# A hybrid encoder trunk on one Trainium2 core: neighbourhood outputs by features, probabilities normalised on GpSimd

## The reference

```python
s = jnp.einsum('brqhd,brkwhd->bhrqkw', qg, k_band).astype(jnp.float32) * (d ** -0.5) + bias
s = jnp.where(in_win[:, None, :], s, -jnp.inf)
p = jax.nn.softmax(s.reshape(B, H, rows, GRID_W, kh * GRID_W), axis=-1).reshape(s.shape)
o = jnp.einsum('bhrqkw,brkwhd->brqhd', p.astype(v.dtype), v_band)
...
mixed = jnp.concatenate([ml_out, na_out, gla_out], axis=-1).astype(h.dtype)
return mixed @ w_out
```

## Time and profile before

| | |
|---|---|
| time, median of 3 runs | 879.58 us (879.28 to 880.8) |
| the profiled execution's own time | 878.24 us |
| its span | 876.3 us |
| TensorE matmul busy | 861.8 us, 98% of the span |
| VectorE busy | 596.0 us, 68% |
| ScalarE busy | 496.1 us, 57% |
| GpSimd busy | 14.3 us, 2% |
| granted TensorE clock, mean | 0.998 of full speed |

### The profile page before, as it was taken

How to read it: one execution, slowest core, us unless ns; L and a number is a source line. 1 busy time by engine, 2 the same in 40 slices (tenths; PEclk the granted TensorE clock), 3 DMA queues, 4 the chain that set the end, 5 groups by cost and what they waited for, 6 DMA issues and landing times.

```text
span 876.3 us, 14948 instructions
## 1 busy us (share of the span) xinstructions
PE 861.8 (98%) x6338; PEld 798.1 (91%) x6338; DVE 596.0 (68%) x820; ACT 496.1 (57%) x689; POOL 14.3 (2%) x35
## 2 busy tenths in 40 slices
PE   8999999999999999999999999999999899999997
PEld 8999998889889999999999999988898899999996
DVE  6887678757657666666577885887665666656655
ACT  7954663658647445445567546745755645445444
POOL 5000000000000000000000000000000000000000
PEclk9999999999999999999999999999999999999999
DMA  9735452364255555555448254335435365555541
GB/s 329 201 102 177 156 178 103 112 226 144 97 193 190 195 190 195 192 191 194 145 140 257 72 171 165 127 115 192 135 109 191 127 212 190 193 196 190 192 169 48
DMA packets 114665, 146.78 MB, mean 168 GB/s; under 512 B 10600, under 2 KB 94760, under 8 KB 114600
## 3 DMA queue, kind: packets, MB, share of 16 engines
q1 hardware_dynamic: 114456, 145.57, 49.7%
q10 hardware_dynamic: 144, 0.26, 0.1%
HBM read 144.77 MB, written 1.05 MB: 166 GB/s over the span
## 4 chain that ended last, share of the span: by engine, by line
PE 92%; ACT 3%; DVE 3%; issue 1%; DMA 0%; ACTq 0%; DVEq 0%
PE bank L665 26%; PE bank L666 25%; PE bank L667 25%; PE bank L706 4%; PE bank L743 2%; PE bank L832 2%; DVE wlo L1455 2%; PE bank L1017 2%; ACT whi L1096 1%; ACT yhi L1119 1%; PE bank L872 1%; PE bank L762 1%; PE bank L849 1%; DVE ylo L1710 1%; PE bank L882 1%
## 5 line engine op out<-in xcount | busy, mean ns | idle before, releaser
L1455 DVE TENSOR_TENSOR wlo<-raw,whi 128x2048 fp32r<-128x2048 f32 (+3 forms) x144 | 306.2, 2133 | 106.1 <-ACT whi L1096 105.2
L1096 ACT ACTIVATE whi<-raw 128x2048 fp32r<-128x2048 f32 (+3 forms) x144 | 257.4, 1793 | 53.5 <-PE bank L667 48.4
L665 PE MATMUL bank<-yhi,whi 128*128 128x256 f32 x704 | 195.1, 277 | 0.5 <-DVE ylo L1471 0.5
L666 PE MATMUL bank<-ylo,whi 128*128 128x256 f32 x704 | 194.6, 276 | 0.0
L667 PE MATMUL bank<-yhi,wlo 128*128 128x256 f32 x704 | 194.6, 276 | 0.0
L665 PEld LDWEIGHTS bank<-yhi,whi 128*128 128x128 f32 x704 | 132.2, 188 | 1.6 <-issue 0.7
L666 PEld LDWEIGHTS bank<-ylo,whi 128*128 128x128 f32 x704 | 132.2, 188 | 0.8
L667 PEld LDWEIGHTS bank<-yhi,wlo 128*128 128x128 f32 x704 | 132.2, 188 | 0.0
L665 PE MATMUL bank<-xhi,whi 128*128 128x256 f32 x320 | 91.4, 286 | 2.2 <-DVE wlo L1455 1.2
L665 PE MATMUL bank<-whi,xhi 128*128 128x512 f32 (+2 forms) x256 | 90.1, 352 | 0.0
L667 PE MATMUL bank<-xhi,wlo 128*128 128x256 f32 x320 | 88.9, 278 | 0.0
(11 more groups left out here) (268 smaller groups left out, 1373.1 us busy)
## 6 DMA issues: line engine op xcount, KB each, us to landing
raw<-in_w_up SPq DMA_DIRECT2D x44, 1024.0 KB, 5.0
raw<-in_w_down SPq DMA_DIRECT2D x22, 1024.0 KB, 4.8
raw<-in_w_in SPq DMA_DIRECT2D x10, 1024.0 KB, 7.3
raw<-in_w_xk SPq DMA_DIRECT2D x8, 1024.0 KB, 5.1
raw<-in_w_xv SPq DMA_DIRECT2D x8, 1024.0 KB, 4.9
raw<-in_w_out SPq DMA_DIRECT2D x8, 1024.0 KB, 4.8
raw<-in_w_xq SPq DMA_DIRECT2D x8, 1024.0 KB, 5.7
raw<-in_w_xo SPq DMA_DIRECT2D x8, 1024.0 KB, 4.9
```

Of the source, the lines that this page charges most:

```text
L665: mm(o, s_hi, m_hi, start=first, stop=False, skip_group_check=True)
L666: mm(o, s_hi, m_lo, start=False, stop=False, skip_group_check=True)
L1096: A(weight(whi, gu), raw[:, gu % RING, 0:SIZE[gu]], ACT.Copy).then_inc(hi_done, 1)
L1455: tt(weight(wlo, gu), raw[:, gu % RING, 0:SIZE[gu]], weight(whi, gu), ALU.subtract).then_inc(lo_done, 1)
```

## The change

A head's output is computed with the operands swapped: the values are the stationary side (64 columns), the transposed probabilities the moving one (256 columns), so that the result has features on the partitions. Two heads share a bank, one on the lower and one on the upper 64 partitions. There are three such groups in place of five: heads 0 and 1 at hh 3, heads 2 and 3 at hh 5, head 4 at hh 6 (`NA_OUT`, `NA_PAIRS`). Each stands ahead of the transposes of its `hh`. Their results are split straight from the bank into `yna_hi` (ScalarE) and `yna_lo` (VectorE), which are operands of the projection for feature groups 3, 4 and the lower half of 5. So groups 3 and 4 are no longer turned through `tmb`, and the projection begins with group 3.

Since a token's sum can no longer be applied per partition of the output, the probabilities are divided before they are transposed. VectorE takes the reciprocal of the sums (`shares_of`), GpSimd multiplies the two halves of the head's probabilities in place (two instructions of 128 by 256), and TensorE's transposes wait for GpSimd (`npn_ready`) where they waited for ScalarE. GpSimd's program after its constants is these 20 multiplications and their waits.

VectorE's order changes too. The mLSTM heads' finish (`heads_sum`) moves from hh 0 to hh 2: ahead of the reciprocals of heads 2 and 3 in layer 0, behind them in layer 1. The unit `xk1` (layer 0) or `xk3` (layer 1) is split at hh 0, ahead of the scores of heads 2 and 3, and on ScalarE it moves ahead of the second `gg` copy. ScalarE's two exponentials for the GLA move from hh 1 to hh 2, behind the heads' own.

```diff
@@ layer_events
     for h in range(NAH + 2):
+        if h in NA_OUT:
+            p = NA_OUT.index(h)
+            job(f"nao{p}", 4 + p % 2)
         if 1 <= h <= NAH:
             job(f"nat{h - 1}", 2 + (h - 1) % 2)
-        if h >= 2:
-            job(f"nao{h - 2}", 4 + (h - 2) % 2)
...
+NA_OUT = (3, 5, 6)
+NA_PAIRS = ((0, 1), (2, 3), (4,))
+NA_K = range(3, 6)
...
+        MIXED_K = (0, 1, 2, 5, 6, 7)
...
@@ gpsimd
+            for l in range(DEPTH):
+                for i in range(NAH):
+                    pool.wait_ge(nsum_ready, NAH * l + i + 1)
+                    for t in range(TT):
+                        last = g.tensor_scalar(np_[:, i % 2, t, :], np_[:, i % 2, t, :], nsum[:, 2 * i + t:2 * i + t + 1], None, ALU.mult)
+                    last.then_inc(npn_ready, 1)
...
@@ tensor
                 for hh in range(NAH + 2):
+                    if hh in NA_OUT:
+                        p = NA_OUT.index(hh)
+                        is_drained(pe, l, f"nat{NA_PAIRS[p][-1]}")
+                        free(f"nao{p}")
+                        for jt in range(TT):
+                            for g in NA_PAIRS[p]:
+                                r = slice(64 * (g % 2), 64 * (g % 2) + 64)
+                                last = mm(bank(f"nao{p}")[r, 0:T], nav[:, jt, g * DH:(g + 1) * DH], npt[:, g % 2, jt].rearrange("p a b -> p (a b)"),
+                                          start=jt == 0, stop=jt == 1, skip_group_check=True)
+                        last.then_inc(te_done, 1)
                     if 1 <= hh <= NAH:
                         g = hh - 1
-                        pe.wait_ge(np_ready, NAH * l + g + 1)
+                        pe.wait_ge(npn_ready, NAH * l + g + 1)
...
-                    if hh >= 2:
-                        g = hh - 2
-                        is_drained(pe, l, f"nat{g}")
-                        free(f"nao{g}")
-                        for t in range(TT):
-                            for jt in range(TT):
-                                last = mm(bank(f"nao{g}")[:, t * DH:(t + 1) * DH], npt[:, g % 2, t, jt, :],
-                                          nav[:, jt, g * DH:(g + 1) * DH], start=jt == 0, stop=jt == 1)
...
                     for k in (i, i + 4):
+                        if k not in MIXED_K:
+                            continue
                         for t in range(TT):
                             last = nc.tensor.transpose(turned_bank(l, "mx", k)[:, t * P:(t + 1) * P], tmb[:, t, k * P:(k + 1) * P], ident[:])
                     last.then_inc(te_done, 1)
-                for n in range(2):
-                    tm_unit(f"wo{n}", (f"wo{n}0", f"wo{n}1"), 512, "mx", n == 0)
+                tm_half("wo0", "a", ("wo00", "wo01"), 512, "mx", True, ks=(3,), first=3, ends=None)
+                tm_half("wo0", "a", ("wo00", "wo01"), 512, "mx", True, ks=(0, 1, 2), first=3, ends=2)
+                tm_half("wo0", "b", ("wo00", "wo01"), 512, "mx", True)
+                tm_unit("wo1", ("wo10", "wo11"), 512, "mx")
...
@@ vector
+                def shares_of(g):
+                    dve.wait_ge(np_ready, NAH * l + g + 1)
+                    V.reciprocal(nsum[:, 2 * g:2 * g + 2], nsum[:, 2 * g:2 * g + 2]).then_inc(nsum_ready, 1)
+
+                def heads_lo(p):
+                    dve.wait_ge(na_hi_ready, 3 * l + p + 1)
+                    r = slice(0, 64 * len(NA_PAIRS[p]))
+                    drain(tt(forwards(yna_lo[r, p, :]), backwards(bank(f"nao{p}")[r, 0:T]), forwards(yna_hi[r, p, :]), ALU.subtract))
...
                     if hh == 2:
+                        if l == 0:
+                            heads_sum()
+                        for g in NA_PAIRS[1]:
+                            shares_of(g)
                         if l:
-                            split_lo("xk3")
+                            heads_sum()
+                        else:
+                            split_lo("xk2")
+                        dve.wait_ge(eb_ready, 2 * l + 2)
...
                         if l == 0:
                             split_lo("xk3")
+                        heads_lo(0)
                     if hh == 4 and l == 0:
                         head_squares(mlh, sq, 0, MLH)
                     if hh == 4:
+                        shares_of(4)
                         split_lo("xv0a")
-                    if hh == 5 and l:
-                        head_squares(mlh, sq, 0, MLH)
+                    if hh == 5:
+                        if l:
+                            head_squares(mlh, sq, 0, MLH)
+                        heads_lo(1)
```

More of the change, by code:

```diff
@@ L335, in build @@
             eg = mixer.enter_context(nc.sbuf_tensor("eg", [P, TT, GV], F32))
+        with ExitStack() as mixer:
+            yna_lo = mixer.enter_context(nc.sbuf_tensor("yna_lo", [P, 3, T], F32R))
         chi = sb("chi", [P, KT, T], F32R)
@@ L712, in fm_unit, with input_is, tm_half @@
                     fm_blocks(name, group, [(f, 0, KT) for f in range(WCOLS[UNIT[l, name]] // P)], fresh, stepped=stepped)
-                def tm_half(unit, half, names, n, group, fresh=False, tokens=(0, 1), ks=range(4)):
+                def input_is(group, kk):
+                    if group == "mx" and kk in NA_K:
+                        is_drained(pe, l, f"nao{kk - 3}")
+                    if group != "mx" or kk in MIXED_K:
+                        lo_is(pe, l, group, kk)
+                def tm_half(unit, half, names, n, group, fresh=False, tokens=(0, 1), ks=range(4), first=0, ends=3):
                     have((l, unit + half))
                     hi, lo = weights((l, unit + half), 4)
-                    x = PAIR[group]
                     for t in tokens:
-                        if half == "a":
+                        if half == "a" and ks[0] == first:
                             free(names[t])
@@ L723, in tm_half @@
                             if fresh and t == 0:
-                                lo_is(pe, l, group, kk)
+                                input_is(group, kk)
                             s = slice(t * P, t * P + P)
+                            x = operand(group, kk)
                             way = from_the_end if unit in ("xv1", "xw1") and t == TT - 1 and kk == KT - 1 else (lambda v: v)
-                            last = split_mm(way(bank(names[t])[:, 0:n]), x[0][:, kk, s], x[1][:, kk, s],
-                                            way(hi[:, k, :]), way(lo[:, k, :]), kk == 0, kk == KT - 1)
-                        if (half == "b" or t == TT - 1) and k == 3:
+                            last = split_mm(way(bank(names[t])[:, 0:n]), x[0][:, s], x[1][:, s],
+                                            way(hi[:, k, :]), way(lo[:, k, :]), kk == first, kk == KT - 1)
+                        if (half == "b" or t == TT - 1) and k == ends:
                             last.then_inc(te_done, 1)
@@ L1271, in _ @@
                         memory_hi("mem", l, range(4, KT))
+                        split_hi("xk3" if l else "xk1")
                         take("gg1")
```

97 lines of the change are left out of this document (47 added, 50 removed).

## The result

| | before | after |
|---|---|---|
| median of the runs, us | 879.43 (879.26 to 880.8, 4 runs) | 892.99 (892.54 to 894.48, 4 runs) |
| ratio to before, 95% interval | | 1.015 [1.0135, 1.0166] |
| profiled execution, us | 878.24 | 892.75 |
| its span, us | 876.3 | 891.0 |
| mean granted clock of TensorE | 0.998 | 0.989 |

What follows compares the result with a forecast made beforehand. TensorE, busy 98% of the span, was taken to bound the kernel. Losses 3.6 + 2.9 less 2 x (0.44 + 0.30) gave +5.0: profiled 878.24 becomes 883.2, median 884.6 us; range 879 to 888.

Steps and rivals of the forecast that it cites:

- three places: TensorE's transposes wait for GpSimd at head 2 in layer 0 (1 to 2 us), head 4 in both layers (about 2 and 5).
- TensorE's saving: Head outputs in the loop: 4.05 us a layer falls to 2.9, saving 1.15; 4.1 in all if nothing new waited.
- The four transposes and the wait for `wo0b`: At the projection, four transposes fewer save 0.44 us a layer and the wait for the split of `wo0b` 0.30.
- The multiplication: GpSimd, ahead of each head's transposes: 0.42 us each, from a select's row; 0.9 for a head's two.
- The hold: A GpSimd instruction started inside a VectorE split (2.2 us) with two SBUF inputs gets nothing done until it is over.
- The walk of VectorE: VectorE's steps through the loop; with GpSimd free, layer 0 gains 0.7 us and layer 1 loses 1.9 at `kt0`.
- +2.9: Layer 0's loop: `kt0` at 142.0 where it was 139.09, a loss of 2.9 us.
- +3.6: Layer 1's loop: `kt0` at 571.8 where it was 568.18, a loss of 3.6 us.
- the free GpSimd: Rival: GpSimd is not held, so 2.2 us behind each split fall away; 879.3 us, chance 0.12.
- a won race: Rival: GpSimd gets a multiplication in ahead of the split, or both ahead of the squares; 882.5 us, chance 0.14.
- The slow multiplication: Rival: a GpSimd multiplication takes 0.85 us, not 0.42, adding 3.3; 888 us, chance 0.13.

Runs made afterwards that it cites:

- experiment 1: The changed kernel without the division: GpSimd's 20 multiplications gone, TensorE's transposes wait for the exponentials; 881.14 us, ratio 1.0021 to the kernel before.
- experiment 8: The changed kernel with the multiplications on VectorE and VectorE's work in another order; 876.16 us, ratio 0.9962 to the kernel before.
- Experiment 7: The changed kernel with each GpSimd multiplication cut to 64 of its 256 columns, so the output differs; 885.74 us, ratio 1.0076 to the kernel before.
- experiment 4: The changed kernel, but VectorE waits for head 2's and head 4's multiplications before it goes on; 887.44 us, ratio 1.0105 to the kernel before.
- experiment 6: The kernel before with only GpSimd's division added and reciprocals early; outputs and other order as before; 900.98 us, ratio 1.0245 to the kernel before.

## Why the prediction was too low

Its direction and its three places were right, and its mechanism as far as it went. What failed is the size of two terms: a wait was priced at its length alone, with nothing for the clock behind it, which measured 4.9 us; and a multiplication was put at 0.42 and measured 0.92, and its hold at what was left of the split, and it lasted longer. The steps, in its order:

**TensorE's saving: right in sum, a little high in the loops and low at the projections.** In experiment 1 layer 0's loop is 0.73 shorter with 0.35 of waiting for the split of `xk2` in it (transposes to `xk2` 0.76 for 0.41), so 1.08 was saved for 1.15. In experiment 8 it is 0.72, its wait left out: the filling ahead of an output group is longer than it was (6 products 0.93 for 0.79, 18 products 2.25 for 2.16), and transposes take 0.53 ahead of scores, where before they took 0.44 ahead of outputs. It seems that a step between products of different tile shapes costs about 0.1 here, which the forecast had near nothing; no run was made for it. Head 4's output takes 1.01, from 148.25 to 149.26, where 0.9 was forecast, and in experiment 8 a pair's takes 1.01 too (123.76 to 124.77; forecast 1.0). The four transposes and the wait for `wo0b` were put at 0.74 a layer; the change shows 1.15 and 1.20. In layer 1 of experiment 8 the twelve transposes take 1.23 to the next product where sixteen took 1.78, that is 0.55 and not 0.44, and the wait of 0.30 had stood in a step of 0.68 between two products that otherwise follow after 0.23, so 0.45 went with it.

**The multiplication: mis-sized.** Priced at 0.42 from a select of the same extent; it takes 0.92. This lies outside the bounds of 0.18 to 0.85 too. A row of another operation with the same shape was no price. Experiment 7 shows what it is made of (0.28 fixed and 2.5 ns a column).

**The hold: right in kind, too short.** Forecast was that GpSimd waits for the split's end (at head 4 of layer 1 for the squares too) and then does both multiplications in 0.9. Head 2 of layer 0 was ready 2.8 after its split's end (124.93 to 127.70). A held multiplication also let VectorE's next instruction ahead of it. Measured from the first scores, the transposes of head 2 come 2.3 later than forecast, those of head 4 in layer 1 0.9 later (32.1 for 31.2). The Trainium skill, "SBUF — State Buffer", section "Who interferes with whom", has the lock go both ways; the trace agrees that VectorE is held too, but by less than a whole multiplication of 0.92: its products beside GpSimd take 0.88 and 0.93 for 0.69, and the eight low parts of the memory 3.69 for 3.25. The latter made TensorE some 0.6 later at head 1 in layer 0 and 0.4 in layer 1; the forecast had nothing for heads 0 and 1.

**The walk of VectorE: right.** Experiment 1 takes GpSimd out and finds -0.73 and +1.6 where the walk had -0.7 and +1.9. In the change itself the bank of `kt0` was ready at 579.2 (low part from 578.82), ahead of the 583.8 at which it was used: behind a wait of 5.26 it no longer bound.

**The clock: missing from the sum.** The prediction priced a wait at its length. After 3.49 and 5.26 TensorE worked for 6 and 5 us at half clock, and the kernel with TensorE kept busy puts this at 3.0 us in layer 0 and 1.9 in layer 1. This is the largest missing term.

So layer 0's loop, +8.65 against +2.9: 2.3 for the late head 2 (0.6 of it from heads 0 and 1), 3.0 for the clock, 0.5 for the longer wait at head 4 (2.72 for 2.2). Layer 1's, +6.55 against +3.6: 0.9 for the late head 4, 1.9 for the clock. The forecast's +5.0, these 5.8 and 2.8, the early start's 1.5 and 0.9 more saved at the projections make +14.2 of the span's +14.7.

Of the rivals, the free GpSimd and a won race didn't happen: at none of the three places did a multiplication come in ahead of its split. The slow multiplication did, and its 888 was the nearest of the figures, and still 5 us too low for want of the clock.

## What to carry to other kernels

Before moving work to an idle engine, see what VectorE does in the very moment at which the work arrives: the same ten pairs of multiplications cost 10 us more than on VectorE where long splits followed directly, and 2 to 3 where short instructions did. Price a new wait on TensorE with what the clock does behind it: here one of 2.20 (with 0.93 shortly before) cost 3.1 more behind it, one of 3.49 cost 3.0 more and one of 5.26 1.9 more, and one of 2.72 nothing. When a change loses, try its parts in another order before giving them up: the outputs by features, with VectorE multiplying, were worth 3 us here, and the change lost 13.6.

## What the runs showed of the hardware

- GpSimd's multiplication of 128 by 256 floats by a value per partition took 0.92 us, of 128 by 64 0.44, against 0.35 on VectorE (0.62 for two) and 0.42 for GpSimd's select of 128 by 256.
- A GpSimd instruction that began inside a VectorE instruction with two SBUF inputs was held for it and sometimes for the next one as well; it then took up to 3.67 us. Between VectorE instructions of 0.69 it got its turn and made some of them 0.2 longer. Eight of 0.4 beside it took 3.69 for 3.25.
- The granted clock around idle stretches of TensorE: at its upper level after 1.15, 1.39, 1.43, 1.76 and one each of 2.48 and 2.72 us; at half for a while after one of 2.03, one of 2.67, after 2.20 and 2.01 that came some 4 us behind another (0.93 and 2.48), and after 3.49, 3.65, 3.82, 3.99, 4.89 and 5.26. The stretches at half were between about 3 and 14 us long; the longest stood behind the 3.82 of experiment 4 and the 3.82 of experiment 6.
- Throwaway products on TensorE ahead of a wait kept the clock at its upper level each time that they were tried, at five places. At three of them it had been at half without them.
